# A hybrid decoder step: the samples' memory steps issued in pairs, key products in four banks

## The chip, the cores and the metric

One core of a Trainium2 chip runs the whole program. The metric is the device time in microseconds (us) of one execution. Three runs of the kernel before gave 851.37, 853.22 and 853.85 us; the median is 853.22.

## The reference, cut to what matters

One inference layer: an mLSTM branch (4 heads of 256) and a forgetting-attention branch (8 heads of 128) side by side, merged by gates, then a mixture of 32 experts. It serves a prompt of 256 tokens and 8 samples of 8 new tokens each. All data are float32. What the change touches is the mLSTM chunk of the samples. For each of 8 samples and 4 heads there is a state C (256 x 256) with a normaliser column n, held together as 256 x 257:

```python
s   = einsum('bhtd,bhsd->bhts', q, k) * w_intra
num = w_inter[..., None] * einsum('bhtd,bhde->bhte', q, C) + einsum('bhts,bhse->bhte', s, v)
C_new = decay_state[..., None, None] * C + einsum('bhs,bhsd,bhse->bhde', w_rows, k, v)
n_new = decay_state[..., None] * n + einsum('bhs,bhsd->bhd', w_rows, k)
```

For each (sample, head): the old state is multiplied by 8 queries, and a new state is the decayed old one plus the product of 8 keys with 8 values. New states are an output.

## The kernel before, in words

TensorE first computes all projections as "dense units". A unit is half of a block of 256 weight columns over 8 slices of the contraction, with each operand split in a high and a low part: 24 matmuls (for a third unit of some blocks 16), into one of banks 0 to 2. The list `SECTIONS` gives the order of the blocks: `mo mk mq mv ga gb fk fq fv bm bf out`, four each. Small stages are hung behind the units by `stages()` (line 76): the list at `(c, u)` names the stages that every engine runs after that unit. Each engine walks the same lists in its own loop and skips stages in which it has no part, so one list sets the order of work on TensorE, ScalarE and VectorE.

Stages around the change, which lie behind the last `ga` unit and the eight `gb` units:

- `SB(h, b)`: one memory step, head h, sample b; n = 8 h + b counts them, 0 to 31. TensorE multiplies the laid-out queries of the sample (`qm`) by the loaded state `Cin[n % 4]`, two column tiles of 64 output rows, into bank 5, which sums over all 8 samples of the head (the query product, L1893). Then it multiplies the sample's masked keys `kwm[n % 2]` (made by ScalarE in `keys_of_step`, L950) by the values, two row tiles of 64, one into bank 6 and one into bank 7 (the key product, L1904). VectorE adds each bank to the decayed old state (L1363, two instructions), signals `cout_full` by a memset (L1365), and the bank is free after its instruction. GpSimd then issues the load of the state of step n + 4 (L663) and the store of the new one (L675).
- At b = 7 TensorE also makes the within-sample product (L1899) into bank 4 between query and key product. VectorE lays the queries of the next head (L1349), and after its step adds the two halves of bank 5 (L1368, which frees the bank) and writes the numerator (L1371).
- `SA(h, 0)`: scores of a head (L1832) into bank 3; VectorE weighs them (L1342); ScalarE copies the head's values and keys (L941, L943).
- `F1`, `F3`, `F2`, `F2H`, `F2L`: norm, gating, transposes and splitting of a finished numerator; for the second prompt tile (t = 1) `F2H` transposes a half into bank 3 (L1873), VectorE gates it (L1322), ScalarE takes the high part (L931), and `F2L` is VectorE's low part (L1329).

In each of these lists the block's own split (ScalarE L798 high part, VectorE L1131 low part, for the block after next) comes after the steps. A bank is handed back and forth by two counts, `bank_full` and `bank_free`; `banks_of(st)` (line 128) lists which banks a stage fills, in the order of the counts, and `claim(st, b)` makes TensorE wait until the fill before has been read. SP only loads weights, gated by finished splits; at the end the expert weights stream in as their slots come free.

Of the kernel before, what the change touches and what calls it, by code (L numbers as in the profile page):

```python
# [31 lines left out]
NS = BS * TS  # L32
# [41 lines left out]
def stages():  # L74

    order = [(c, u) for c in range(NCH) for u in range(units_of(c))]
    at = {cu: [] for cu in order}

    def after(section, chunk, unit, n=0):

        return at[order[order.index((CPS * SECTIONS.index(section) + chunk, unit)) + n]]

    for n in range(1, 6):
        after("mo", 0, 1, 1 + 3 * (n - 1)).append(("G", n, 0))
    for t in range(3):
        after("mq", 1 + t, 1).append(("KT", t, 0))

    for h in range(HM):
        after("mv", h, 2, 2 if h < HM - 1 else 1).append(("P2", 0, h))
        after("mv", h, 2).append(("P1", 0, h))  # L90
    after("ga", 0, 0).append(("F1", 0, 0))
    for h in range(HM):
        after("ga", 1, 1, h).append(("P2", 1, h))
        after("ga", 0, 1, h).append(("P1", 1, h))
    after("ga", 0, 1).append(("F3", 0, 0))
    after("ga", 1, 0).append(("F2", 0, 0))

    after("ga", 2, 1).append(("SA", 0, 0))
    after("ga", 3, 0).append(("F1", 1, 0))
    for h in range(HM):  # L100
        for b in range(BS):
            line = after("ga", 3, 1, (h * BS + b) * 9 // (HM * BS))
            line.append(("SB", h, b))
            if h == 0 and b in (4, 5, 6):
                line.extend({4: (("F2H", 1, 0),), 5: (("F2L", 1, 0), ("F2H", 1, 1)), 6: (("F2L", 1, 1),)}[b])
        if h < HM - 1:
            line.append(("SA", h + 1, 0))
    after("ga", 3, 1).append(("F3", 1, 0))
    after("fk", 0, 0).append(("F1", 2, 0))
    after("fk", 0, 1).append(("F3", 2, 0))  # L110
    after("fk", 1, 0).append(("F2", 2, 0))

    for w, section in enumerate(("fk", "fq")):
        for t in range(3):
            after(section, 3, 2, 2 * t).append(("N1", w, t))
            after(section, 3, 2, 2 * t + 3).append(("N2", w, t))

    after("fv", 2, 2).append(("FS0", 0, 0))
    for n in range(HF + 2):
        line = after("fv", 3, 0, n) if n else after("fv", 2, 2)  # L120
        line.extend((k, n - s, 0) for s, k in ((2, "FS3"), (1, "FS2"), (0, "FS1"), (-1, "FS0")) if 0 <= n - s < BS)
        line.extend((k, n - s, 0) for s, k in ((2, "FP3"), (1, "FP2"), (0, "FP1")) if 0 <= n - s < HF)
        if n >= 2:
            line.append(("FS4", n - 2, 0))
    return at


def banks_of(st):

    kind, x, y = st  # L130
    if kind == "G":
        return {1: (3,), 2: (4, 5, 6), 3: (3, 7), 4: (3, 7, 4, 5, 6), 5: (3,)}[x]
    if kind == "P2":
        return (4, 6, 7) if x == 0 else (5, 4, 6, 7)
    if kind == "SB":
        return ((5, 4) if y == BS - 1 else ()) + (6, 7)
    return {"KT": (6, 7), "P1": (3,), "F1": (), "F3": (), "F2": (6, 7), "F2H": (3,), "F2L": (), "SA": (3,), "N1": (), "N2": (6, 7),
            "FP1": (7, 4), "FP2": (5,), "FP3": (6,), "FS1": (3,), "FS2": (5,), "FS3": (4,), "FS4": (3,), "FS0": ()}[kind]


# [17 lines left out]
def hybrid_step(nc, A, O):  # L158
# [10 lines left out]
    with ctx:  # L169
        handles = {}  # L170

        def sem(name):
            if name not in handles:
                
                handles[name] = ctx.enter_context(nc.semaphore(name))
            return handles[name]
# [600 lines left out]
        def _(act):  # L777
# [158 lines left out]
            def SA(st):  # L936
                h = st[1]
                n = 2 * HM + h
                pe_past(("P2", 1, HM - 2 + h) if h < 2 else ("SB", h - 2, BS - 1))
                act.wait_ge(sem("low_added"), n_low(first("mv") + h + 1))  # L940
                s(A_(vx2[NS:2 * NS, h, :], vx2[0:NS, h, :], ACT.Copy))  # L941
                for k in range(2):
                    s(A_(kw[n % 2][NS * k:NS * (k + 1), 0:P], kM(2, h)[:, P * k:P * (k + 1)], ACT.Copy,  # L943
                         scale=ew[0:NS, 2, 8 + h:9 + h]), sem("kw_ready") if k else None)
                keys_of_step(h * BS)

            def keys_of_step(n):
                if n >= 2:
                    pe_past(("SB", (n - 2) // BS, (n - 2) % BS))
                s(A_(kwm[n % 2][:, 0:P], kw[n // BS % 2][:, 0:P], ACT.Copy, scale=blk8[:, n % BS:n % BS + 1]),  # L950
                  sem("kwm_ready"))

            def SB(st):
                _, h, b = st
                if b < BS - 1:
                    keys_of_step(h * BS + b + 1)
                else:
                    got(st, 5)
                    act.wait_ge(sem("inter_used"), HM + h)
                    s(A_(inter[0:NS, :], bank[5][NS:2 * NS, 0:DE], ACT.Copy), sem("inter_upper"))  # L960
# [150 lines left out]
        def _(dve):  # L1111
# [207 lines left out]
            def gated(st, i, b):  # L1319
                t = st[1]  # L1320
                got(st, b)
                done(TT(cube(hv, 4)[:, :, 0:ROWS[t]], cube(bank[b][:, :], 4)[:, :, 0:ROWS[t]], sgm[half_of_gates(t, i)],  # L1322
                        ALU.mult), b)
                s(v.memset(small[0:1, 94:95], 0.0), sem("hv_full"))
# [4 lines left out]
                s(TT(r2[1][w], cube(hv, 4)[:, :, 0:ROWS[t]], r2[0][w], ALU.subtract), sem("ha_split"))  # L1329

            def F2H(st):
                gated(st, st[2], 3)

            def F2L(st):
                gate_lo(st[1], st[2])
# [16 lines left out]
            def SB(st):  # L1352
                _, h, b = st
                n = h * BS + b
                if n >= NCOUT:

                    dve.wait_ge(sem(f"cout_out{n % NCOUT}"), 16 * (n // NCOUT))
                if b == BS - 1 and h < HM - 1:
                    got(st, 5)
                    lay_queries(h + 1)  # L1360
                for k, bk in enumerate((6, 7)):
                    got(st, bk)
                    done(STT(Cout[n % NCOUT][:, k, :], Cin[n % NCIN][:, k, :], dec8[:, HM * b + h:HM * b + h + 1],  # L1363
                             bank[bk][:, 0:DE], ALU.mult, ALU.add), bk)
                s(v.memset(small[0:1, 94:95], 0.0), sem("cout_full"))  # L1365
                if b == BS - 1:
                    dve.wait_ge(sem("inter_upper"), h + 1)
                    TT(inter[0:NS, :], bank[5][0:NS, 0:DE], inter[0:NS, :], ALU.add).then_inc(sem("bank_free5"), 1)  # L1368
                    dve.wait_ge(sem("bank_free5"), fill[st, 5] + 1)
                    got(st, 4)  # L1370
                    done(STT(num[0:NS, h, :], inter[0:NS, :], ew[0:NS, 2, h:h + 1], bank[4][0:NS, 0:DE],  # L1371
                             ALU.mult, ALU.add), 4)
                    s(v.memset(small[0:1, 94:95], 0.0), sem("num_full"))
                    s(v.memset(small[0:1, 94:95], 0.0), sem("inter_used"))
# [319 lines left out]
        def _(pe):  # L1694
# [3 lines left out]
            def claim(st, b):  # L1698

                if fill[st, b]:  # L1700
                    pe.wait_ge(sem(f"bank_free{b}"), fill[st, b])
# [173 lines left out]
                full(ins, b)  # L1875

            def F2H(st):
                gate_turns(st, st[2], 3)

            def SA(st):  # L1880
                _, h, _ = st
# [3 lines left out]
            def SB(st):  # L1885
                _, h, b = st
                n = h * BS + b
                if b == 0:
                    claim(("SB", h, BS - 1), 5)
                    pe.wait_ge(sem("qm_full"), 2 * (h + 1))  # L1890
                pe.wait_ge(sem(f"cin_in{n % NCIN}"), 16 * (n // NCIN + 1))
                for k in range(2):
                    ins = mm(bank[5][NS * k:NS * (k + 1), 0:DE], qm[:, 576 * k + 64 * b:576 * k + 64 * (b + 1)],  # L1893
                             Cin[n % NCIN][:, k, :], start=(b == 0), stop=(b == BS - 1), skip_group_check=True)
                if b == BS - 1:
                    full(ins, 5)
                    pe.wait_ge(sem("bank_free3"), fill[("SA", h, 0), 3] + 1)
                    claim(st, 4)
                    full(mm(bank[4][0:NS, 0:DE], SW[(2 * HM + h) % 2][0:NS, 0:64], vx(2, h), start=True, stop=True), 4)  # L1899
                pe.wait_ge(sem("kwm_ready"), n + 1)  # L1900
                for k, bk in enumerate((6, 7)):
                    claim(st, bk)
                    rows = slice(NS * k, NS * (k + 1))
                    full(mm(bank[bk][:, 0:DE], kwm[n % 2][rows, 0:P], vx2[rows, h, :], start=True, stop=True), bk)  # L1904
# [333 lines left out]
```

## Time and profile before

| | |
|---|---|
| median of three runs | 853.22 us |
| the profiled execution | 851.17 us |
| its span | 849.3 us |
| TensorE busy | 738.6 us, 87% |
| VectorE busy | 403.8 us, 48% |
| ScalarE busy | 298.3 us, 35% |
| GpSimd busy | 144.2 us, 17% |
| TensorE's mean granted clock | 0.965 of full |

The span is the time from the first to the last instruction. Busy times of different engines overlap. The chain that ended last names, step by step back from the end, the work on which the next thing waited; its shares say where the time lies, while busy shares only say how much each engine did. The memory steps lie between 205.5 and 288.4 us.

### The profile page before, as it was taken

How to read it: one execution, taken by the hardware profiler on the slowest of the kernel's cores; microseconds unless marked ns; L12 is line 12 of the kernel's file. 1: busy time of each engine (PE TensorE's matmuls, PEld its weight loads, DVE VectorE, ACT ScalarE, POOL GpSimd, SP SyncE). 2: the span in 40 equal slices, each digit the busy share in tenths (PEclk: the TensorE clock that was granted, in tenths of full speed). 3: DMA queues.
4: the chain of work that ended last, by engine and by line, in shares of the span. 5: the costliest groups of instructions: out<-in, count | busy, mean ns of one | idle time of the engine just before them, and what ended most of it. 6: DMA issues, size and time to landing. Idle time of an engine off the chain costs nothing.

```text
span 849.3 us, 14573 instructions
## 1 busy us (share of the span) xinstructions
PE 738.6 (87%) x5476; PEld 592.1 (70%) x5476; DVE 403.8 (48%) x936; ACT 298.3 (35%) x550; POOL 144.2 (17%) x245
## 2 busy tenths in 40 slices
PE   2999899999999999987789999893899999777770
PEld 1799899998666798986678889882755555443430
DVE  3476233565755457584456657746642222111123
ACT  4532644465533445563222234544311111111110
POOL 5001000002433200421212100003012222212210
PEclk9999999999999999999999999997899999999995
DMA  5244343334889632736566538856399999999976
GB/s 189 100 150 144 142 141 108 102 105 183 247 247 255 219 108 104 257 101 208 178 223 227 162 109 304 352 232 237 155 421 418 419 418 418 420 419 419 419 304 193
DMA packets 38170, 202.84 MB, mean 239 GB/s; under 512 B 7490, under 2 KB 8018, under 8 KB 18898
## 3 DMA queue, kind: packets, MB, share of 16 engines
q1 hardware_dynamic: 24434, 160.29, 49.3%
q0 software_dynamic: 13664, 41.58, 15.5%
q8 instruction: 46, 0.75, 0.4%
q14 instruction: 26, 0.21, 0.1%
HBM read 184.24 MB, written 23.38 MB: 244 GB/s over the span
## 4 chain that ended last, share of the span: by engine, by line
PE 60%; DMA 18%; DVE 11%; ACT 5%; issue 4%; SPq 1%; POOLq 0%; DVEq 0%; POOL 0%; ACTq 0%
PE bank L1742 20%; PE bank L1746 10%; DMA fm<-in_w_moe 7%; DMA em<-in_w_moe 7%; PE bank L2096 6%; PE bank L1732 3%; PE bank L2116 3%; DVE rm L1131 2%; PE bank L1904 2%; ACT rm L798 2%; PE bank L1988 2%; PE bank L2077 2%; PE bank L1893 1%; DMA fm<-y_rows 1%; DMA fm<-in_w_dense 1%
## 5 line engine op out<-in xcount | busy, mean ns | idle before, releaser
L1742 PE MATMUL bank<-rm 128*128 128x320 f32 x1344 | 206.0, 312 | 2.6 <-ACT fm L826 1.6
L1742 PEld LDWEIGHTS bank<-rm 128*128 128x128 f32 x1344 | 197.4, 188 | 7.0 <-issue 3.1
L1131 DVE TENSOR_TENSOR rm<-fm,rm 128x2048 fp32r<-128x2048 f32 x48 | 110.0, 2292 | 71.8 <-ACT rm L798 71.2
L1746 PE MATMUL bank<-rm 128*128 128x256 f32 x960 | 122.3, 287 | 2.4 <-DVE fm L1522 2.4
L1746 PEld LDWEIGHTS bank<-rm 128*128 128x128 f32 x960 | 118.4, 194 | 3.3 <-issue 2.9
L798 ACT ACTIVATE rm<-fm 128x2048 fp32r<-128x2048 f32 x48 | 91.9, 1915 | 19.0 <-PE bank L1742 11.1
L2098 PE MATMUL bank<-fm,em 128*64 128x256 f32 x384 | 96.6, 397 | 0.0
L2096 PE MATMUL bank<-em 128*64 128x256 f32 x272 | 68.1, 395 | 13.4 <-DMA fm<-in_w_moe 7.9
L2096 PE MATMUL bank<-fm,em 128*64 128x256 f32 x240 | 58.9, 390 | 10.6 <-DMA fm<-in_w_moe 9.2
L2096 PEld LDWEIGHTS bank<-em 128*64 128x64 f32 x272 | 36.2, 141 | 40.4 <-issue 25.3
L1094 ACT ACTIVATE fm<-bank 64x256 f32<-64x256 f32 x32 | 12.0, 375 | 136.7 <-PE bank L2098 136.7
L732 POOL DMA_INDIRECT y_rows<-fm,im x32 | 29.2, 913 | 161.7 <-DVE fm L1648 157.4
L2096 PEld LDWEIGHTS bank<-fm,em 128*64 128x64 f32 x240 | 31.6, 139 | 33.5 <-issue 18.7
L2098 PEld LDWEIGHTS bank<-fm,em 128*64 128x64 f32 x384 | 51.4, 141 | 0.0
L663 POOL DMA_DIRECT2D fm<-in_state_C x32 | 17.6, 551 | 164.4 <-DVE fm L1284 119.1
L1653 DVE TENSOR_TENSOR fm<-bank,fm 64x256 f32<-64x256 f32 x32 | 13.6, 426 | 61.7 <-ACT fm L1094 61.6
L1732 PE MATMUL bank<-rm 128*128 128x256 f32 x320 | 42.9, 286 | 0.0
L1363 DVE SCALAR_TENSOR_TENSOR fm<-fm,bank 128x257 f32<-128x257 f32 x64 | 28.0, 479 | 30.4 <-PE bank L1904 29.5
L1660 DVE COPY fm<-bank 128x128 f32<-128x128 f32 x32 | 9.3, 291 | 68.3 <-PE bank L2107 68.2
L1732 PEld LDWEIGHTS bank<-rm 128*128 128x128 f32 x320 | 40.0, 192 | 1.6 <-DVE fm L1522 1.5
L1648 DVE COPY fm<-bank 64x512 f32<-64x512 f32 x32 | 22.2, 694 | 29.5 <-PE bank L2116 29.5
L1087 ACT ACTIVATE fm<-bank 64x512 f32<-64x512 f32 x32 | 18.9, 589 | 44.7 <-PE bank L2116 44.7
(391 smaller groups left out, 1013.4 us busy)
## 6 DMA issues: line engine op xcount, KB each, us to landing
fm<-in_w_moe SPq DMA_DIRECT2D x57, 1024.0 KB, 26.8
fm<-in_w_dense SPq DMA_DIRECT2D x48, 1024.0 KB, 4.9
em<-in_w_moe SPq DMA_DIRECT2D x39, 1024.0 KB, 26.0
fm<-in_state_C POOLq DMA_DIRECT2D x32, 257.0 KB, 5.4
out_C_sample<-fm POOLq DMA_DIRECT2D x32, 257.0 KB, 6.5
fm<-in_cache_v POOLq DMA_DIRECT2D x16, 512.0 KB, 4.5
fm<-in_cache_kT POOLq DMA_DIRECT2D x10, 512.0 KB, 5.8
em<-in_cache_kT POOLq DMA_DIRECT2D x6, 512.0 KB, 7.9
```

Of the source, the lines that this page charges most:

```text
L732: pool.indirect_dma_start(y_rows, bass.IndirectOffsetOnAxis(ap=row_i[:, v:v + 1].bitcast(U32), axis=0), yrow[v % NY], None, bounds_check=6 ...
L798: s(A_(pair[c % 2][0], cube(raw[c % RAW1], KC), ACT.Copy), sem("hi_done"))
L1087: A_(yrow[v % NY][:, 0:D // 2], bank[4 + v % 2][0:CAP, :], ACT.Copy).then_inc(sem("e_y_left"), 1)
L1131: s(TT(pair[c % 2][1], cube(raw[c % RAW1], KC), pair[c % 2][0], ALU.subtract), sem("split_done"))
L1363: done(STT(Cout[n % NCOUT][:, k, :], Cin[n % NCIN][:, k, :], dec8[:, HM * b + h:HM * b + h + 1], bank[bk][:, 0:DE], ALU.mult, ALU.add), bk)
L1648: CP(yrow[v % NY][:, D // 2:D], bank[4 + v % 2][CAP:2 * CAP, :]).then_inc(sem("e_y_right"), 1)
L1732: ins = mm(bank[b][:, 0:CW], samp[:, k, :], w[:, k, :], start=(k == 0 and i == 0), stop=(k == KC - 1 and i == 1))
L1742: ins = mm(bank[b][:, 0:NT], w[:, k, P * u:P * (u + 1)], a[:, k, :], start=first, stop=final)
L1746: ins = mm(bank[b][0:r, 0:CW], a[:, k, TILE0[u]:TILE0[u] + r], w[:, k, :], start=first, stop=final)
L2096: last_g = mm(bank[b][0:CAP, 0:FE], x[:, k, :], g[:, k, :], start=(k == 0), stop=(k == KC - 1), skip_group_check=True)
L2098: last_u = mm(bank[b][CAP:2 * CAP, 0:FE], x[:, k, :], u[:, k, :], start=(k == 0), stop=(k == KC - 1), skip_group_check=True)
L2116: ins = mm(bank[b][CAP * j:CAP * (j + 1), :], hT[:, k, :], w[:, k, 512 * j:512 * (j + 1)], start=(k == 0), stop=(k == 1), skip_group_check ...
```

## The change

Three edits that hang together:

1. In the lists, the two steps of a pair (b even and b + 1) now always stand behind the same dense unit. TensorE runs the query products of both at the even step; the odd step has only its key product. At the end of a head the sum in bank 5 and the within-sample product thus come at b = 6, ahead of both last key products.
2. Key products use banks 6 and 7 for even steps, 3 and 4 for odd ones, and 3 and 6 for b = 7.
3. The scores and copies of the next head (`SA`) come after b = 3 and not after b = 7; the masked keys of a head's first step are made by the step before it. `F2H` moves ahead of the step b = 4 with its first half, its second half uses bank 4.

```diff
-            line = after("ga", 3, 1, (h * BS + b) * 9 // (HM * BS))
+            line = after("ga", 3, 1, (h * BS + b // 2 * 2) * 9 // (HM * BS))
+            if h == 0 and b == 4:
+                line.append(("F2H", 1, 0))
             line.append(("SB", h, b))
-            if h == 0 and b in (4, 5, 6):
-                line.extend({4: (("F2H", 1, 0),), 5: (("F2L", 1, 0), ("F2H", 1, 1)), 6: (("F2L", 1, 1),)}[b])
-        if h < HM - 1:
-            line.append(("SA", h + 1, 0))
+            if h == 0 and b in (4, 5):
+                line.extend({4: (("F2L", 1, 0), ("F2H", 1, 1)), 5: (("F2L", 1, 1),)}[b])
+            if h < HM - 1 and b == 3:
+                line.append(("SA", h + 1, 0))
...
+KEY_BANKS = [(6, 7), (3, 4)] * 3 + [(6, 7), (3, 6)]
...
     if kind == "SB":
-        return ((5, 4) if y == BS - 1 else ()) + (6, 7)
+        return ((5, 4) if y == BS - 1 else ()) + KEY_BANKS[y]
+    if kind == "F2H":
+        return (3 + y,)
...
-                keys_of_step(h * BS)
+                if h == 0:
+                    keys_of_step(0)
...
-                if b < BS - 1:
+                if h * BS + b + 1 < HM * BS:
                     keys_of_step(h * BS + b + 1)
-                else:
+                if b == BS - 1:
...
-                pe.wait_ge(sem(f"cin_in{n % NCIN}"), 16 * (n // NCIN + 1))
-                for k in range(2):
-                    ins = mm(bank[5][NS * k:NS * (k + 1), 0:DE], qm[:, 576 * k + 64 * b:576 * k + 64 * (b + 1)],
-                             Cin[n % NCIN][:, k, :], start=(b == 0), stop=(b == BS - 1), skip_group_check=True)
-                if b == BS - 1:
+                for c in (b, b + 1) if b % 2 == 0 else ():
+                    m = h * BS + c
+                    pe.wait_ge(sem(f"cin_in{m % NCIN}"), 16 * (m // NCIN + 1))
+                    for k in range(2):
+                        ins = mm(bank[5][NS * k:NS * (k + 1), 0:DE], qm[:, 576 * k + 64 * c:576 * k + 64 * (c + 1)],
+                                 Cin[m % NCIN][:, k, :], start=(c == 0), stop=(c == BS - 1), skip_group_check=True)
+                if b == BS - 2:
                     full(ins, 5)
                     pe.wait_ge(sem("bank_free3"), fill[("SA", h, 0), 3] + 1)
-                    claim(st, 4)
+                    claim(last, 4)
                     full(mm(bank[4][0:NS, 0:DE], SW[(2 * HM + h) % 2][0:NS, 0:64], vx(2, h), start=True, stop=True), 4)
                 pe.wait_ge(sem("kwm_ready"), n + 1)
-                for k, bk in enumerate((6, 7)):
+                for k, bk in enumerate(KEY_BANKS[b]):
```

With this the steps behind the nine units are 0-3, 4-7, 8-11, 12-15, 16-17, 18-21, 22-25, 26-29, 30-31; before they are 0-3, 4-7, 8-10, 11-14, 15-17, 18-21, 22-24, 25-28, 29-31.

## Rows read from the trace of the kernel before

**Rows 1.** The page: busy time of TensorE, and the chain's shares.
```profile
PE 738.6 (87%) x5476; PEld 592.1 (70%) x5476; DVE 403.8 (48%) x936; ACT 298.3 (35%) x550; POOL 144.2 (17%) x245
...
PE 60%; DMA 18%; DVE 11%; ACT 5%; issue 4%; SPq 1%; POOLq 0%; DVEq 0%; POOL 0%; ACTq 0%
PE bank L1742 20%; PE bank L1746 10%; DMA fm<-in_w_moe 7%; DMA em<-in_w_moe 7%; PE bank L2096 6%; PE bank L1732 3%; PE bank L2116 3%; DVE rm L1131 2%; PE bank L1904 2%; ACT rm L798 2%; PE bank L1988 2%; PE bank L2077 2%; PE bank L1893 1%; DMA fm<-y_rows 1%; DMA fm<-in_w_dense 1%
```

**Rows 2.** Stretches: length, busy PE, PEld, DVE, ACT, POOL, clock, DMA share, GB/s.
```profile
205.47:288.33 82.86, 78.90 (x477) 51.18 (x476) 46.63 (x135) 33.92 (x63) 32.00 (x59) 1.00 0.86 255
...
211.36:223.10 11.74, 11.02 (x71) 6.95 (x71) 10.74 (x28) 7.61 (x13) 5.04 (x10) 1.00 0.87 257
223.10:231.22 8.12, 7.95 (x50) 5.52 (x48) 3.80 (x15) 3.51 (x8) 2.61 (x6) 1.00 0.96 233
231.22:240.95 9.73, 9.45 (x57) 6.23 (x57) 5.79 (x14) 3.14 (x6) 4.33 (x9) 1.00 0.87 247
240.95:251.01 10.06, 8.76 (x56) 5.81 (x55) 4.37 (x17) 4.37 (x9) 3.25 (x7) 1.00 0.89 273
251.01:260.67 9.66, 9.49 (x57) 6.31 (x57) 5.78 (x14) 2.84 (x6) 4.33 (x9) 1.00 0.79 242
260.67:270.19 9.52, 8.70 (x55) 5.80 (x55) 4.13 (x16) 4.48 (x9) 3.96 (x8) 1.00 0.89 241
270.19:279.86 9.67, 9.50 (x59) 6.31 (x57) 5.92 (x14) 2.72 (x6) 3.62 (x7) 1.00 0.93 260
279.86:288.33 8.47, 8.29 (x51) 5.49 (x50) 2.50 (x9) 2.25 (x5) 2.34 (x5) 1.00 0.66 223
```

**Rows 3.** The chain of waits in a clean stretch: start, length, what.
```profile
251.08 3.72 PE bank L1742 x24
254.80 0.58 PE bank L1893 x4
255.38 0.64 PE bank L1904 x3
...
256.14 0.49 DVE fm L1363
...
256.77 1.00 PE bank L1904 x4
```

**Rows 4.** The timeline at a head's end, ScalarE and VectorE.
```profile
246.28 0.84 ACT L943 ACTIVATE fm<-fm 64x128 f32<-64x128 f32 x2
...
246.63 0.87 DVE L1363 SCALAR_TENSOR_TENSOR fm<-fm,bank 128x257 f32<-128x257 f32 x2 [0.74 <-PE bank L1904]
...
247.56 0.42 DVE L1368 TENSOR_TENSOR fm<-bank,fm 64x257 f32<-64x257 f32 x1
```

**Rows 5.** The chain of waits elsewhere: five products of TensorE.
```profile
200.73 0.43 PE bank L1855 x2
...
216.37 0.60 PE bank L1873 x4
...
222.80 0.38 PE bank L1832 x4
...
245.32 0.57 PE bank L1899 x2
...
444.55 1.90 PE bank L1953 x16
```

**Rows 6.** The timeline in the second stretch, VectorE.
```profile
214.31 2.29 DVE L1131 TENSOR_TENSOR rm<-fm,rm 128x2048 fp32r<-128x2048 f32 x1 [0.24 <-DVE fm L1307]
...
217.57 0.69 DVE L1322 TENSOR_TENSOR fm<-bank,fm 128x512 f32<-128x512 f32 x1
```

**Rows 7.** Loads of the state (L663): whole program, then 229 to 243 us.
```profile
  PEld bank L1893: 0.5, 1
...
DMA to landing us min/median/max: 3.4/5.4/7.5
...
DMA to landing us min/median/max: 3.4/6.8/7.3
```

More of the change, by code:

```diff
@@ L135, in banks_of @@
     if kind == "SB":
-        return ((5, 4) if y == BS - 1 else ()) + (6, 7)
-    return {"KT": (6, 7), "P1": (3,), "F1": (), "F3": (), "F2": (6, 7), "F2H": (3,), "F2L": (), "SA": (3,), "N1": (), "N2": (6, 7),
+        return ((5, 4) if y == BS - 1 else ()) + KEY_BANKS[y]
+    if kind == "F2H":
+        return (3 + y,)
+    return {"KT": (6, 7), "P1": (3,), "F1": (), "F3": (), "F2": (6, 7), "F2L": (), "SA": (3,), "N1": (), "N2": (6, 7),
             "FP1": (7, 4), "FP2": (5,), "FP3": (6,), "FS1": (3,), "FS2": (5,), "FS3": (4,), "FS4": (3,), "FS0": ()}[kind]
@@ L1331, in F2H @@
             def F2H(st):
-                gated(st, st[2], 3)
+                gated(st, st[2], 3 + st[2])
             def F2L(st):
@@ L1877, in F2H @@
             def F2H(st):
-                gate_turns(st, st[2], 3)
+                gate_turns(st, st[2], 3 + st[2])
             def SA(st):
@@ L1887, in SB @@
                 n = h * BS + b
+                last = ("SB", h, BS - 1)
                 if b == 0:
-                    claim(("SB", h, BS - 1), 5)
+                    claim(last, 5)
                     pe.wait_ge(sem("qm_full"), 2 * (h + 1))
-                pe.wait_ge(sem(f"cin_in{n % NCIN}"), 16 * (n // NCIN + 1))
-                for k in range(2):
-                    ins = mm(bank[5][NS * k:NS * (k + 1), 0:DE], qm[:, 576 * k + 64 * b:576 * k + 64 * (b + 1)],
-                             Cin[n % NCIN][:, k, :], start=(b == 0), stop=(b == BS - 1), skip_group_check=True)
-                if b == BS - 1:
+                for c in (b, b + 1) if b % 2 == 0 else ():
[5 more added lines that the diff above has]
+                if b == BS - 2:
                     full(ins, 5)
                     pe.wait_ge(sem("bank_free3"), fill[("SA", h, 0), 3] + 1)
-                    claim(st, 4)
+                    claim(last, 4)
                     full(mm(bank[4][0:NS, 0:DE], SW[(2 * HM + h) % 2][0:NS, 0:64], vx(2, h), start=True, stop=True), 4)
                 pe.wait_ge(sem("kwm_ready"), n + 1)
-                for k, bk in enumerate((6, 7)):
+                for k, bk in enumerate(KEY_BANKS[b]):
                     claim(st, bk)
```

## The prediction

> **What bounds the kernel now.** I read the page's busy row and chain first [rows 1]: TensorE is busy 87% of the span and owns 60% of the chain of waits; the expert weights' transfers own 14%, all at the end. Then the busy times by stretch [rows 2]. The edit lies between 205.47 us (first memory step) and 288.33 us (first `fk` unit), 82.86 us, in which TensorE is busy 78.90 at full granted clock, VectorE 46.63, ScalarE 33.92, GpSimd 32.00; the transfer engines are 86% busy. So TensorE's program order sets the time here, and the transfers come next. What lies behind is started by events of TensorE (units done, slots used), the expert weights too, so I pass a change of this stage to the end one for one.
>
> The stage is nine runs of steps with eight dense units between them. A clean dense unit takes 3.72 us: its 24 matmuls start at 251.08 and the next query product at 254.80 [rows 3]. A step's query product takes 0.58 us of TensorE, its key product 0.64 if both banks are free [rows 3]. The clean stretch 251.01 to 260.67 has one unit and four steps, 3.72 + 4 x 1.22 = 8.60, but takes 9.66: 1.06 is waiting. The chain shows on whom: key product at 255.38, VectorE starts on its bank 0.76 later (I use 0.80, from the start), and 0.63 after VectorE's start (256.14 to 256.77) the next key product starts, on the first bank alone; the second follows, so it takes 1.00 and not 0.64 [rows 3]. In all: 8 x 3.72 + 32 x 1.22 + 4 x 0.57 (within-sample products) + 3 x 0.38 (scores) + 2 x 0.60 (transposes of F2H) [rows 5] = 73.4; so 9.4 of 82.86 are waits or lost overlap. That is what can be won.
>
> **What the change removes and adds.** The counts of all products, evacuations and transfers stay; two copies per head change place. I walk TensorE through the nine stretches with these prices:
> - Step of VectorE: 0.94 from one to the next if nothing holds it (246.63 to 247.56 [rows 4]). It frees its first bank 0.63 after its start, its second at about 1.01.
> - Second of two query products back to back. The trace of before has no such pair. Bounds: 0.58 as today, and 0.43, the time of two instructions of the full array and the same width [rows 5]. The nearest row is FS1: sixteen instructions of 264 columns in two alternating column tiles in 1.90 us, 0.475 per four [rows 5]. Scaled to 257 columns: 0.46. I take 0.46, and for the second key product 0.50 (bounds 0.43 and 0.64).
> - Scores in mid-head: 0.38, but they claim bank 3, which the step before (odd, banks 3 and 4) has just filled. From the key product of step 2 VectorE needs 0.80 + 0.94 + 0.63 = 2.37 until that bank is free.
> - Last step of a head: banks 3 and 6. Bank 6 was filled by step 6, so from step 6's key product: 0.80 + 0.63 = 1.43, then 0.55 for a half product alone: 1.98 where 1.14 would do.
>
> The walk; a clean pair is 0.58 + 0.46 + 0.64 + 0.50 = 2.18.
> 1. Steps 0 to 3: 2.18, then 1.04, wait 2.37, scores 0.38: 5.97. Before 5.89 (205.47 to 211.36 [rows 2]; so for the others).
> 2. Steps 4 to 7: unit 3.72, turn 0.60, queries 1.04, key 4 at 5.36, turn to 6.60. Step 5 needs bank 4, which the second turn filled. VectorE: its 2.29 us split ended 5.24 into this stretch; ScalarE now does the next head's three copies (0.84 for two [rows 4], 1.26) ahead of its table load, and that load starts 0.70 later against the unit than today, so the split ends at 5.94. Then gating 0.69, a memset, step 4 (0.94), the low half 0.69, gating 0.69 [rows 6]: 9.1, with gaps and signal 9.3. Key 5 ends at 9.85. Queries 1.04, within-sample 0.57, keys 1.98: 13.44. Before 11.74.
> 3. Steps 8 to 11 and scores: 3.72 + 5.97 = 9.69. Before 8.12 with three steps.
> 4. Steps 12 to 15: 3.72 + 2.18 + 1.04; the within-sample product claims bank 4 of step 13, free at 3.72 + 1.04 + 0.80 + 0.94 + 1.01 = 7.51; 0.57; 1.98: 10.06. Before 9.73.
> 5. Steps 16, 17: 3.72 + 2.18 = 5.90. Before 10.06 with three steps, the scores and the head's edge.
> 6. Steps 18 to 21, scores between: 3.72 + 1.04 + 2.37 + 0.38 + 2.18 = 9.69. Before 9.66.
> 7. Steps 22 to 25, a head's edge inside: key 22 at 3.72 + 1.04 + 0.57 = 5.33. Bank 5 is free after 0.80, step 0.94, query copies 0.45, step 0.94, sum 0.42, 0.14: at 9.02; then 2.18: 11.20. Before 9.52.
> 8. Steps 26 to 29: 3.72 + 4.36 = 8.08. Before 9.67.
> 9. Steps 30, 31: 3.72 + 1.04 + 0.57 + 1.98 = 7.31. Before 8.47.
> Sum 81.34 against 82.86: **-1.5 us**. The clean stretches win 1.6 each; scores in mid-head, the head's last step, the turn in bank 4 and the one head's edge without a dense unit behind it give most of it back.
>
> **Loads of the state.** Four buffers: the load of step n+4 is issued once VectorE has finished step n. Today loads land 3.4 to 7.5 us after issue, 5.4 in the median, and TensorE waits 0.5 for one of them [rows 7]. In a clean stretch of today the need comes 9.66 - 0.58 - 0.80 - 0.94 - 0.3 (GpSimd's start) = 7.0 after issue. In the walk the odd step's query product comes earlier and its buffer doesn't. Example, step 17: VectorE ends step 13 at 3.72 + 1.04 + 0.80 + 0.94 + 0.94 = 7.44 of stretch 4, GpSimd issues at 7.9 (it still issues step 12's store), and the need is 10.06 - 7.9 + 3.72 + 0.58 = 6.5 later; loads of that time took up to 7.3 [rows 7], so it waits 0.8. In the same way step 9 has 6.8 where 7.5 was needed (0.7), step 10 has 5.8 + 0.7 against 6.8 (0.3), step 31 has 4.6 against 5.4 (0.8); today's wait stays (0.4). Sum 3.0, less the 0.5 that is there already: **+2.5**. Bounds: -0.5 (every load in time) and +4.2 (each 0.5 us slower, felt at three or four places, as the engines are 86% busy already).
>
> The Trainium skill (DMA: Bandwidth & Descriptors, Anatomy of one DMA) fits a transfer on GpSimd's path as about 2.0 us plus the bytes at 436 GB/s. For 257 KB an estimate by that page is 2.6 us, the loads would all be in time and the sum would be -2.0. The trace doesn't agree: 5.4 in the median [rows 7], with stores and dense weights on the same engines, so I go by the rows.
>
> **Sum.** -1.5 + 2.5 = +1.0 us on the profiled execution's 851.17 (span 849.3, 1.9 around it): 852.2. That execution lies 2.0 below the median of the runs shown; the same difference on the median 853.22 gives 854.2. A measurement of this kernel tells 0.3%, 2.6 us, from no change; this is within it. Costs taken as nothing: ScalarE's masked copies (0.4 each, like those in [rows 4]) keep ahead of the key products, since each needs only the product two steps back; without that cover a pair would lose some 0.2. GpSimd's queue has the same 60 issues.
>
> The 0.12 and 0.14 that I gain at each second product also follow from a rule of the Trainium skill (TensorEngine Tiling (Array Packing), Key Properties): changing the tiling mode drains TensorE. Query products use column tiles, key products row tiles, so pairing halves the changes. The rule gives no price, and no run so far shows such a pair.
>
> **Rivals.**
> - Loads in time and part of the new waits absent (faster). For: only one load wait today, and my bank waits are stacked one on the other. Against: walked with the same prices, today's clean stretch comes out at 9.6, and is 9.66 [rows 2]. The new bank waits of the walk are 3 x 1.2 (scores), 4 x 0.8 (last steps) and 2.6 (turn in bank 4), 9.4; with a fifth of them gone, -1.5 - 0.5 - 2.0 = -4.0: 849.2. Chance 0.22.
> - The state's transfers decide (slower). Place: the odd query product of a pair, behind which the even step's key product, ready long ago, is queued. It decides where a load takes over some 6 us. Each 0.5 us more of latency costs 1.7: +4.2 - 1.5 = +2.7 at 0.5 more, +4.4 at 1.0; I take +4.0: 857.2. For: 86% busy, latencies up to 7.5. Against: the stage has no more bytes than before and, waiting, gives them time. Chance 0.18.
> - Back-to-back products gain nothing (slower): the 16 second queries lose 0.12 and the eight second keys that nothing else holds 0.14, so +3.0 on the forecast: +4.0, also 857.2. Against: the FS1 row. Chance 0.12.
> - The forecast: 0.48, its own range 851.5 to 856.5.
>
> Faster is the first rival, 0.22; slower the second and third, 0.30; same 0.48. The range for 8 in 10 takes most of both sides: 850.0 to 858.0.
>
> **What would show it.** Right: the eighth stretch at 8.1 for four steps; scores starting about 2.4 after the key product of step 2; the key product of a head's last step taking 1.3 or more; the stretch of steps 4 to 7 longer than 13; three or more waits of query products for `in_state_C`, together 2 to 3 us; in pairs a second query product 0.46 behind the first. Wrong: a stage of 79 or less (the new waits are not there), or over 86 with load waits above 4; a change of more than 1 us outside the stage would make passing it on one for one wrong.

## The result: slower, 863.96 us, and the profile after

Four runs of the changed kernel gave 858.92, 863.43, 864.49 and 867.66 us, median 863.96, against 852.5 for the kernel before beside it: a ratio of 1.0128, 95% interval 1.0086 to 1.0169. The forecast was 854.2, range 850.0 to 858.0. The profiled execution took 864.49, 13.3 more than the 851.17 of before: the stage begins 1.25 earlier, is 13.65 longer, and what lies behind it takes 561.9 for 561.0. The earlier begin need not come of the change: the profiles of runs in the order of before begin the stage between 203.4 and 205.5.

In the page TensorE's busy time has grown by 4.9 with the same 5476 matmuls [rows 1]:

```profile
PE 743.5 (86%) x5476; PEld 597.9 (69%) x5476; DVE 406.0 (47%) x936; ACT 298.5 (35%) x550; POOL 143.9 (17%) x245
...
PE 57%; DMA 19%; DVE 12%; ACT 5%; issue 5%; SPq 1%; POOL 1%; POOLq 0%; DVEq 0%; ACTq 0%
```

The stretches after (columns as in [rows 2]), first the whole stage, then the nine behind the nine units. The last columns are granted clock, DMA share and GB/s.

```profile
204.22:300.73 96.51, 82.43 (x478) 56.55 (x477) 48.94 (x136) 35.20 (x63) 31.33 (x58) 0.88 0.73 219
204.22:210.00 5.78, 4.88 (x38) 2.80 (x37) 4.49 (x16) 3.35 (x9) 2.70 (x6) 1.00 0.90 314
210.00:226.21 16.21, 14.31 (x68) 8.69 (x67) 10.75 (x28) 8.30 (x12) 4.27 (x8) 0.76 0.81 245
226.21:236.85 10.64, 9.77 (x61) 7.60 (x61) 5.34 (x18) 3.36 (x9) 4.34 (x9) 0.88 0.52 134
236.85:252.50 15.65, 11.66 (x60) 7.12 (x58) 6.11 (x16) 4.25 (x7) 4.29 (x9) 0.79 0.85 246
252.50:259.90 7.40, 7.40 (x41) 6.29 (x40) 1.92 (x8) 1.06 (x3) 1.67 (x4) 0.76 0.52 143
259.90:269.25 9.35, 8.19 (x62) 6.19 (x60) 6.31 (x15) 5.18 (x10) 4.33 (x8) 1.00 0.63 194
269.25:283.33 14.08, 11.03 (x60) 6.90 (x59) 5.58 (x20) 2.83 (x8) 4.33 (x8) 0.88 0.78 240
283.33:293.42 10.09, 8.11 (x58) 5.79 (x57) 5.67 (x13) 3.56 (x6) 4.33 (x8) 1.00 0.71 226
293.42:300.73 7.31, 7.07 (x45) 5.17 (x43) 2.78 (x10) 3.30 (x5) 1.08 (x2) 1.00 0.72 206
```

The walk had 5.97, 13.44, 9.69, 10.06, 5.90, 9.69, 11.20, 8.08, 7.31. Where the clock is 1.00 and no load is waited for (first, sixth, ninth) it holds within 0.4. The excess stands in the other six, and two things share it. One is late loads: TensorE's waits in the stage (engine, line, releaser: us, times, longest) have 7.1 us for `in_state_C`. The kernel before has no such wait of a product, only one of a weight load, 0.5 [rows 7]; weight loads wait 9.3 here.

```profile
PE bank L1904 <- DMA fm<-in_state_C: 7.1, 4, 3.2
PE bank L1840 <- DVE fm L1371: 2.9, 3, 1.2
PE bank L1904 <- DVE fm L1376: 1.7, 1, 1.7
PE bank L1915 <- ACT fm L958: 1.4, 1, 1.4
```

The timeline shows the longest being made. GpSimd issues four loads (L670) and four stores (L682) back to back; the fourth load, step 15's, is the one that step 15's query product (L1904) waits for:

```profile
234.11 0.55 POOL L670 DMA_DIRECT2D fm<-in_state_C  x1 [5.79 <-DVE fm L1373]
...
237.40 0.55 POOL L670 DMA_DIRECT2D fm<-in_state_C  x1
237.94 0.54 POOL L682 DMA_DIRECT2D out_C_sample<-fm  x1
...
243.54 0.65 PE L1904 MATMUL bank<-fm 128*64 128x257 f32 x4 [0.82 <-DMA fm<-in_state_C]
...
247.36 1.12 PE L1904 MATMUL bank<-fm 128*64 128x257 f32 x4 [3.16 <-DMA fm<-in_state_C]
```

The trace's landing time of that one load alone:

```profile
DMA to landing us min/median/max: 9.9/9.9/9.9
```

The other is TensorE's clock. The last row of the timeline has four matmuls in 1.12 us, where the row above it has step 14's same four in 0.65. Windows of 2 us show the granted clock fall in or behind a pause (in each the busy time of TensorE stands behind the length, the clock third from the end):

```profile
216.00:218.00 2.00, 0.63 (x5) 0.39 (x5) 1.85 (x6) 1.03 (x2) 0.16 (x1) 1.00 0.66 113
218.00:220.00 2.00, 1.47 (x4) 0.62 (x4) 1.51 (x4) 0.76 (x2) 0.93 (x2) 0.63 0.95 242
220.00:222.00 2.00, 2.00 (x9) 0.77 (x8) 1.23 (x3) 0.68 (x2) 0.72 (x2) 0.50 0.92 380
...
246.00:248.00 2.00, 0.64 (x4) 0.30 (x4) 0.00 (x0) 0.00 (x0) 0.00 (x0) 0.50 0.87 308
248.00:250.00 2.00, 2.00 (x8) 0.79 (x6) 0.00 (x0) 0.00 (x0) 0.00 (x0) 0.50 0.96 390
```

0.50 is 1.2 GHz, 1.00 is 2.4 GHz. The fall comes three times in the stage: from 218.6 to 228.9 (behind a pause of 1.4 us and in one of 0.5), from 245.8 to 256.2 (it falls within the load wait of 3.2), from 279.8 to 283.4 (behind the head's edge, 1.7). The stage of before is at 1.00 throughout.

### The profile page after: what moved, and what is told of

Read it like the earlier page. It is cut to its first block, busy times and chain, and to the rows that moved or that the text cites. A ratio compares the mean times of both kernels' runs of the same rounds, so it can differ in the third digit from the quotient of the medians.

```text
span 862.6 us, 14573 instructions
## 1 busy us (share of the span) xinstructions
PE 743.5 (86%) x5476; PEld 597.9 (69%) x5476; DVE 406.0 (47%) x936; ACT 298.5 (35%) x550; POOL 143.9 (17%) x245
## 4 chain that ended last, share of the span: by engine, by line
PE 57%; DMA 19%; DVE 12%; ACT 5%; issue 5%; SPq 1%; POOL 1%; POOLq 0%; DVEq 0%; ACTq 0%
PE bank L1750 19%; PE bank L1754 10%; DMA fm<-in_w_moe 7%; DMA em<-in_w_moe 7%; PE bank L2107 6%; PE bank L1740 3%; PE bank L2127 3%; DMA fm<-in_state_C 3%; DVE rm L1139 3%; ACT rm L805 2%; PE bank L1915 2%; PE bank L1999 2%; PE bank L2088 2%; PE bank L1904 1%; DMA fm<-y_rows 1%
## 5 line engine op out<-in xcount | busy, mean ns | idle before, releaser
L1750 PE MATMUL bank<-rm 128*128 128x320 f32 x1344 | 208.8, 314 | 2.6 <-ACT fm L833 1.6
L2109 PE MATMUL bank<-fm,em 128*64 128x256 f32 x384 | 98.1, 401 | 0.0
L2107 PE MATMUL bank<-fm,em 128*64 128x256 f32 x240 | 63.1, 410 | 14.2 <-DMA fm<-in_w_moe 12.8
L2107 PE MATMUL bank<-em 128*64 128x256 f32 x272 | 65.3, 383 | 8.4 <-DMA fm<-in_w_moe 4.8
L2107 PEld LDWEIGHTS bank<-fm,em 128*64 128x64 f32 x240 | 33.1, 146 | 38.8 <-issue 24.2
L2109 PEld LDWEIGHTS bank<-fm,em 128*64 128x64 f32 x384 | 51.8, 142 | 0.0
L670 POOL DMA_DIRECT2D fm<-in_state_C x32 | 17.5, 548 | 177.5 <-DVE fm L1292 119.1
```

What stands on the lines that cost most here:

```text
L1750: ins = mm(bank[b][:, 0:NT], w[:, k, P * u:P * (u + 1)], a[:, k, :], start=first, stop=final)
L2107: last_g = mm(bank[b][0:CAP, 0:FE], x[:, k, :], g[:, k, :], start=(k == 0), stop=(k == KC - 1), skip_group_check=True)
L2109: last_u = mm(bank[b][CAP:2 * CAP, 0:FE], x[:, k, :], u[:, k, :], start=(k == 0), stop=(k == KC - 1), skip_group_check=True)
```

## The experiments

The table has, for the profiled execution, the stretch from the first query product to the first `fk` unit, and all executions' median. "Pauses" are those of TensorE of 1.2 us or more in the stage, with a star where the clock fell to 0.50 in the pause or within 3 us behind it. The ratio is to the runs of the kernel before that were timed beside each run (medians 852.4 to 852.8), not to the 853.22 of the first row.

| kernel | stage us | PE busy | clock | DMA | pauses | median (range) | ratio to before, interval |
|---|---|---|---|---|---|---|---|
| before | 82.86 | 78.90 | 1.00 | .86 | none | 853.22 (851.4-853.9) | |
| after | 96.51 | 82.43 | .88 | .73 | 1.4* 3.2* 1.7* 2.0 | 863.96 (858.9-867.7) | 1.0128, 1.0086-1.0169 |
| e1 | 84.18 | 73.82 | .98 | .86 | 1.4 1.2* 1.7 | 856.00 (850.6-863.1) | 1.0046, 1.0011-1.0082 |
| e2 | 88.64 | 81.33 | .90 | .81 | 1.3* 2.4* 1.2* | 854.44 (852.2-857.1) | 1.0025, 1.0008-1.0041 |
| e3 | 87.81 | 82.34 | 1.00 | .81 | none | 860.55 (859.7-864.5) | 1.0109, 1.0072-1.0145 |
| e4 | 82.79 | 78.93 | 1.00 | .86 | none | 852.29 (850.6-854.3) | 1.0006, 0.9991-1.0020 |
| e5 | 87.47 | 79.74 | .92 | .80 | 2.8* 3.5* | 854.85 (852.3-857.7) | 1.0019, 1.0003-1.0034 |
| e6 | 86.36 | 77.27 | .98 | .84 | 2.4 2.3* | 854.96 (847.5-858.7) | 1.0017, 0.9992-1.0042 |
| e7 | 83.03 | 78.83 | 1.00 | .84 | none | 852.53 (850.4-854.0) | 0.9993, 0.9977-1.0009 |
| e8 | 87.58 | 80.90 | .96 | .81 | 2.8* | 858.83 (858.6-860.1) | 1.0075, 1.0047-1.0103 |
| e9 | 80.53 | 72.29 | 1.00 | .90 | 1.4 1.7 | 854.65 (849.1-861.2) | 1.0030, 1.0003-1.0058 |
| e10 | 80.50 | 76.22 | .98 | .89 | 1.7* | 847.48 (843.7-850.9) | 0.9942, 0.9920-0.9964 |
| e11 | 80.52 | 72.30 | 1.00 | .53 | 1.4 1.7 | 851.51 (847.8-854.4) | 0.9985, 0.9961-1.0008 |
| e12 | 82.82 | 78.96 | 1.00 | .50 | none | 851.27 (850.0-853.4) | 0.9993, 0.9979-1.0008 |
| e13 | 77.10 | 74.32 | 1.00 | .56 | none | 846.01 (844.9-846.3) | 0.9927, 0.9907-0.9946 |
| e14 | 83.64 | 76.35 | .99 | .87 | 2.4* | 855.49 (852.9-861.0) | 1.0041, 1.0022-1.0059 |
| e15 | 85.36 | 80.02 | .98 | .83 | 1.5* | 855.18 (853.6-857.9) | 1.0044, 1.0025-1.0064 |
| e16 | 80.76 | 75.63 | 1.00 | .51 | none | 851.35 (849.0-854.0) | 0.9982, 0.9967-0.9996 |
| e17 | 78.11 | 74.08 | 1.00 | .87 | none | 848.17 (847.0-849.9) | 0.9950, 0.9933-0.9968 |

**e1, e4: six state buffers**, in the changed kernel and in the one before.

```diff
-NCIN, NCOUT = 4, 4
+NCIN, NCOUT = 6, 4
...
-            s(CP(dg[0:16, 0, 0:NT], bank[7][0:16, 0:NT]), sem("gates_taken"))
+            s(CP(dg[0:16, 0, 0:NT], bank[7][0:16, 0:NT]), sem("wg_split"))
```

(Not shown: the new buffers' places in memory. Two early counts, `gates_taken` and `lfn_ready`, give up their semaphores. All runs with more buffers have this.)

> The changed kernel with six buffers for the loaded states in place of four, so that a load is issued two steps earlier. In the changed kernel the memory stage takes 96.5 us, with 8.0 us of waits of query products for loads, and the granted clock of TensorE in it is 0.88 in the mean (0.50 in three spells). Theory A (pauses of TensorE, of whatever cause, are followed by spells at half clock, and these are the larger part of the loss): load waits go to under 1 us, the spell at 246 us goes with its pause, the one at 218 us, which follows a wait for the transposes' bank, stays; stage 83 to 87 us, whole 850 to 856 us. Rival B (the new waits on banks alone are the loss): the loads don't matter, 861 to 865 us. Rival C (the clock falls for a reason outside the stage, such as heat or the other work of the chip): load waits go, the clock stays near 0.88, 856 to 859 us.

> The kernel before with six buffers for the loaded states. It waits once for a load, 0.5 us. All theories: 852 to 854 us, stage 82.3 to 83 us, clock 1.00. If it gains more than 2 us, loads bound the stage in a way that the waits don't show, and the first kernel's reading is wrong.

e4 takes the time of the kernel before: loads don't bound it. In e1 no load is late and the median falls by 8 of the 11.5 that were lost, so most of the loss hung on late loads (its A, at the upper end). One thing of A missed: the pause of 1.4 at step 5 stayed, and no spell at half clock came behind it. What comes in place of late loads is late stores; VectorE's waits:

```profile
DVE fm L1372 <- DMA out_C_sample<-fm: 7.4, 2, 5.0
```

**e2: the four key banks alone**, in the order of before: `KEY_BANKS = [(6, 7), (3, 4)] * 3 + [(6, 7), (6, 7)]`.

> The kernel before with one part of the change alone: odd steps' key products in banks 3 and 4, but b = 7 in banks 6 and 7; the order of products, steps and scores as before. Theory A: clean stretches of four steps shrink from 9.66 to about 8.7 us, no pause over 1.5 us, clock stays 1.00, stage 79 to 81 us, whole 849 to 851.5 us. Rival B (four banks bring waits on banks 3 and 4 that cost what they save): stage 82 to 85, whole 852 to 856. Rival D (the loads bind once steps are faster): stage 81 to 84 with load waits of 2 us or more.

Each clean four-step group loses its bank waits (4.88 us from 204.20 to 209.08), yet the stage grows: 3.2 us of waits for `in_state_C` and three stretches at half clock. Theory D had the load waits, none the clock.

**e3: the changed kernel with twenty idle identity products in its five pauses.**

> The changed kernel with idle products (identity times a constant table, 256 columns, 0.43 us each, overwritten by the next real product) put into five of its pauses: 3 ahead of the key product of step 5, 7 between the query products of steps 14 and 15, 2 between 22 and 23, 4 between 28 and 29, 4 ahead of step 24; 20 in all, 8.7 us of work that is of no use. Theory A (idle pauses bring the half clock): the clock in the stage is 0.97 or more, stage 86 to 89 us, whole 853 to 857 us, though TensorE has more to do. Rival B or a loss that comes of the waits alone: the products at best fill pauses, stage 96 to 99 us, whole 864 to 867 us. Rival C (clock falls for another reason): as B.

The clock of the stage is 1.00 and the stage is 8.7 shorter, as A had it; the whole is only 3.4 better and missed A's range, since behind the stage it took 566.2 for 561.9.

**e5, e6: both cures together**, other banks with six buffers, and pairs with six buffers and idle products (`mm(bank[b][:, 0:256], ident, negs, ...)`).

> The order of the kernel before (no pairs, scores and copies at the head's edge), with six state buffers instead of four, and key products of odd steps in banks 3 and 4 wherever TensorE made no extra pause of over 1 us for them: steps 4 to 7 of the first head and every head's last step stay in banks 6 and 7. Theory A (TensorE loses time beyond its own waits where a pause of 1 us or more is followed by half the granted clock; short bank waits only cost themselves): no pause over 1 us is left but the turn of the first head, granted clock of the stage 0.98 or more, stage 76 to 79.5 us, whole 846 to 850. Theory B (the banks bring nothing, since VectorE's pace takes the place of TensorE's waits): stage 81.5 to 83.5, whole 851.5 to 854. Theory C (the loads again): query products wait for in_state_C over 2 us in sum, whole 852 or more.

> The changed kernel with six state buffers, and seven idle identity products of 256 columns into banks 3 and 7, three ahead of the key product of step 5 and four ahead of step 24, so that TensorE is at work in the two places where it paused for over 1 us. Their results are not used. Theory A (the changed kernel's excess over the walk is half clock after pauses, and late loads): with both gone the stage is 82 to 85 us at a granted clock of 0.98 or more, whole 851.5 to 855. Theory B (the walk itself was too short: pairs, scores in mid-head and the head's last step cost more than their waits): stage 86 or more at full clock, whole 856 or more.

No theory of e5 fits: its stage is 87.47, with no wait of TensorE for a load. Of e6 the median is in A's range, its stage of 86.36 is not. Both fail at one place, the store. VectorE's waits in e5 and, second, in e6:

```profile
DVE fm L1353 <- DMA out_C_sample<-fm: 5.1, 1, 5.1
DVE fm L1367 <- DMA out_C_sample<-fm: 1.5, 2, 0.9
```

```profile
DVE fm L1372 <- DMA out_C_sample<-fm: 14.2, 3, 6.4
```

With loads far ahead, a step waits until the state of four steps ago is stored. In e5 TensorE then pauses 2.8 and 3.5 us, and the clock falls with each; in e6 it pauses 2.4 and 2.3, and the clock falls only at the second.

**e7, e15, e8: one pause of TensorE alone**, in e4's kernel, by 3, 5 and 7 copies on ScalarE ahead of step 20's masked keys.

```diff
+                if (h, b) == (2, 3):
+                    for _ in range(3):
+                        s(A_(hv, hv, ACT.Copy))
```

> The kernel before with six state buffers and three copies of a masked half onto itself added on ScalarE (0.6 us each) ahead of the masked copies of step 20, so that one key product of TensorE comes about 2 us late, in a stage that runs at full granted clock otherwise. Theory A (a pause of 1 to 3 us may be followed by some 10 us at half the granted clock): in the executions in which that happens the time rises by the pause and some 4 to 5 us more, in the others by the pause alone; the profile shows 0.50 in the windows behind it, or nothing; whole 853 to 859, with more spread than before. Theory B (a pause costs its own length and no clock): whole 852.5 to 855 in every run, clock 1.00 behind the pause.

> The kernel before with six state buffers and five copies on ScalarE ahead of step 20's masked copies; three made no pause of TensorE beyond 0.2 us, seven made one of 2.8. Here it is about 1.5. Theory A (a pause of this size is followed by half clock in some executions and not in others): the executions fall around 853 to 854 (852.3 and the pause less what the next wait gives back) and around 857, the median between. Theory B (it takes over 2 us of pause): all at 852.5 to 855.

> As the run with three copies, with seven: one pause of TensorE of about 4.4 us. Theory A: the half clock behind it comes in more of the executions, or in all: whole 857 to 863, of which 4.4 is the pause. Theory B: 855.5 to 858, the pause alone, clock 1.00 behind it. If the time is that of the run with three copies, the copies are hidden behind something and the run says nothing on the clock.

Three copies make no pause (0.17) and cost nothing, so e7 tells nothing of the clock. Five make one of 1.50 and cost 2.8 over before; the seven executions lie at 853.6 to 855.2 (four) and 857.4 to 857.9 (three). Seven copies make one of 2.82 and cost 6.3, in all four executions. Of e8, TensorE's timeline behind the pause and two windows in it:

```profile
259.63 1.23 PE L1908 MATMUL bank<-fm 64*128 64x257 f32 x4 [2.82 <-ACT fm L952]
260.79 1.13 PE L1897 MATMUL bank<-fm 128*64 128x257 f32 x4
```

```profile
256.00:258.00 2.00, 0.81 (x6) 0.20 (x4) 0.88 (x3) 1.91 (x4) 1.65 (x4) 1.00 0.85 262
...
260.00:262.00 2.00, 2.00 (x10) 0.59 (x8) 0.88 (x3) 0.42 (x2) 0.00 (x0) 0.50 0.57 210
```

Against e4 the profiled stage is 2.57 longer in e15 (1.09 of it is busy time) and 4.79 longer in e8 (1.97 of it busy), so within the stage a pause cost 1.7 times its length. By the medians it is 1.8 and 2.2 times; the rest lies outside the stage and was not traced to the pause. Nor are e15's two groups those with and without the fall: the profiled execution, 855.13, is of the lower group and has it. This is the only place where one pause was varied with order and transfers as they were.

**e9, e10: five buffers for loads and five for stores**, for the changed kernel and for the order of before with the other banks.

```diff
-NCIN, NCOUT = 4, 4
+NCIN, NCOUT = 5, 5
+KEY_BANKS = [[(6, 7), (3, 4)] * 2 + [(6, 7)] * 4] + [[(6, 7), (3, 4)] * 3 + [(6, 7), (6, 7)]] * 3
```

(`KEY_BANKS` in e10 alone. Not shown: the list of slots, in which a store's buffer is not always n % 5, and a wait of ScalarE for the last store from the fifth.)

> The changed kernel with five buffers for loaded states and five for states to be stored (before: four and four). With six and four, VectorE waited up to 5 us for a store (out_C_sample) ahead of a step and TensorE then paused over 1 us. Theory A (late loads and late stores make the long pauses, and half clock follows some of them): waits for in_state_C and out_C_sample together under 3 us, stage 82 to 86 us, whole 852 to 857. Theory B (the fifth buffer only moves the wait, since the transfers can't follow in this stage): waits for transfers of 4 us or more in sum, stage 86 or more, whole 857 or more.

> The order of the kernel before, key products of odd steps in banks 3 and 4 except at a head's last step and steps 4 to 7, and five buffers each for loads and stores. With six and four this had two pauses of 2.8 and 3.5 us behind waits for stores and lost 6.8 us to the half clock behind them; without both its stage would be 76 to 77. Theory A: the fifth output buffer takes most of these waits away: stage 76 to 80, whole 846.5 to 850. Theory B (the stage's transfers can't be done in less than about the 82.8 us of before, the buffers only shift where it is felt): stage 82 to 86, whole 852 to 856, with waits for transfers of 4 us or more.

e9's profile has one wait of VectorE for a store left, 4.4 us, hidden from TensorE, and a stage of 80.53 at full clock, shorter than both theories; its median is in A's range. Its executions spread from 849 to 861, the longer ones at a lower mean clock (0.959 for 849.1, 0.949 for 861.2). e10's median is A's, its stage of 80.50 just above; it is 5 us faster than before and the fastest of the kernels that move whole states. Against e10 the pairs and what goes with them (e9) cost 7.2 us in the median. Five and five buffers in the kernel before alone were not run.

**e11, e12, e13: half of every state moved**, with four buffers each; the changed kernel, the kernel before, and the other banks.

```diff
+                w = slice(0, 1 if n >= NCIN else 2)
-                pool.dma_start(Cin[n % NCIN], A["state_C"][n % BS, n // BS])
+                pool.dma_start(Cin[n % NCIN][:, w], A["state_C"][n % BS, n // BS][:, w])
```

> The changed kernel with half of every state loaded and stored from step 4 on (the other half is left out of the outputs; all products and evacuations stay). Theory A (late transfers cause the load waits, and they and the pause of step 5 the spells at half clock): no wait for in_state_C, stage 81 to 85.5 us (the walk of 81.3, with at most one spell behind the pause of 1.4 us at step 5), whole 850 to 855. Theory B (the order of the products itself is slow): stage 88 or more, whole 857 or more.

> The same with the kernel before, as its control. TensorE sets its stage and no transfer is late in it: stage 82.3 to 83, whole 851.5 to 853.5, by both theories. If it comes out faster by over 1 us, transfers held the kernel before as well.

> The kernel before with four buffers each, key products of odd steps in banks 3 and 4 except at a head's last step and steps 4 to 7, and half of every state loaded and stored from step 4 on (the other half is missing in the outputs). Theory A (only late transfers held the other banks back): no wait for a transfer, stage 80 to 81 us as with five buffers each, whole 845 to 849. Theory B (the fifth buffers did something else): stage 82 or more, whole 850 or more.

With its program order untouched and less to move, the changed kernel has no transfer wait and its median is 12.5 us lower, so it was slow by transfers that come late under its order, and not by the order's own length. That of the kernel before is 1.2 lower, by its expectation a sign that transfers held it too; but its stage is the same (82.82), and the interval takes in no change. e11's stretches, the DMA share now 0.53:

```profile
204.09:284.61 80.52, 72.30 (x478) 51.65 (x477) 48.97 (x136) 35.21 (x63) 31.34 (x58) 1.00 0.53 174
204.09:209.85 5.76, 4.89 (x38) 2.92 (x37) 4.50 (x16) 3.35 (x9) 2.68 (x5) 1.00 0.88 333
209.85:223.13 13.28, 11.14 (x69) 7.42 (x67) 10.28 (x27) 8.29 (x12) 3.79 (x8) 1.00 0.63 211
223.13:232.62 9.49, 8.62 (x61) 6.45 (x60) 5.82 (x19) 3.36 (x9) 4.83 (x9) 1.00 0.25 86
232.62:242.82 10.20, 9.20 (x61) 6.34 (x59) 5.64 (x15) 4.25 (x7) 3.81 (x8) 1.00 0.67 219
242.82:248.62 5.80, 5.80 (x42) 4.70 (x41) 2.41 (x9) 1.07 (x3) 2.16 (x4) 1.00 0.39 113
248.62:257.97 9.35, 8.18 (x63) 6.19 (x61) 6.31 (x15) 5.18 (x10) 4.33 (x8) 1.00 0.57 190
257.97:269.13 11.16, 9.22 (x61) 6.34 (x59) 5.15 (x19) 2.43 (x7) 4.33 (x8) 1.00 0.47 118
269.13:277.31 8.18, 8.18 (x59) 6.14 (x57) 6.39 (x15) 4.14 (x7) 3.53 (x7) 1.00 0.52 176
277.31:284.61 7.30, 7.06 (x44) 5.16 (x43) 2.48 (x9) 3.13 (x4) 1.88 (x4) 1.00 0.40 142
```

e13 shows what the banks alone are worth when nothing is late: a stage of 77.10, 5.7 under e12's (and shorter than its A), and 5.3 in the median. The changed kernel under the same terms (e11) is 3.4 longer in the stage and 5.5 in the median: its reordering costs more than it gives.

**e14, e16: idle products in the pauses** at step 5 and at step 24, in e9's and in e11's kernel.

> The changed kernel with five buffers each and seven idle identity products of TensorE, three ahead of the key product of step 5 and four ahead of step 24, in its two pauses of 1.4 and 1.7 us. Theory A (the half clock in most executions of the run without them comes from these pauses): stage 80.5 to 82 in the profile, whole 847 to 851, and a smaller spread than 849.1 to 861.2. Theory B (the half clock has nothing to do with the pauses): median 853 to 856 and the same spread as without.

> The changed kernel with half of every state loaded and stored from step 4 on (the other half is missing in the outputs), so that no transfer is late, and the seven idle products of TensorE, three ahead of the key product of step 5 and four ahead of step 24. Without them the executions lay at 847.8 to 848.3, 851.0 to 852.9 and 854.0 to 854.4, median 851.5, by the mean granted clock of each. Theory A (the pauses of 1.4 and 1.7 us bring the half clock of the upper two groups): all executions at 847.5 to 850. Theory B (the half clock comes from elsewhere): the same groups and a median of 851 to 853.

e14 came out in B's range but says little: a 6.8 us wait for a store is back and makes a pause of 2.4. e16 went by B: no pause over 1.2 is left in its stage, and the executions still lie at 849.0 to 854.0. So the spread of e11 doesn't come from those two pauses.

**e17: e10 with stores issued ahead of loads.**

> The order of before with the other key banks and five buffers each (847.5 us), with each store issued ahead of the load of five steps later and not behind it. Theory A (a store lands later by what the load ahead of it takes, the loads have time to spare with five buffers): waits of VectorE for out_C_sample under 1 us in sum, whole 845 to 848. Theory B (the loads now come late instead): waits for in_state_C over 1 us, whole 848 to 852.

No store is waited for, one load for 0.9, the stage is 2.4 shorter than e10's in the profile, but the whole is the same: 848.17 against 847.48, the ranges overlap.

## Why the prediction was wrong

- **The walk held.** With no transfer late, e11's stage has 80.52 for the forecast 81.34; its stretches 5.76, 13.28, 9.49, 10.20, 5.80, 9.35, 11.16, 8.18, 7.30 lie within 0.35 of it each. Scores start 2.28 behind the key product of step 2 (2.4 forecast); a pair of query products takes 1.02 and one 0.58, so the second 0.44; a pair of key products 1.07 and one 0.64, so 0.43 (0.46 and 0.50 forecast). The rival "gains nothing" falls. One cost taken as nothing, ScalarE's masked keys, did show: the pause of 1.37 ahead of step 5 ends with them (L958). It hid behind the wait for bank 4, 0.53 more, so the length came out right; but it is the pause right behind which the clock first fell in the changed kernel.
- **Of the -1.5 nothing reached the median.** e11 against e12 is 851.5 to 851.3, though the profiled stages differ by 2.3. Passing the stage on one for one was too simple: behind it the 19 profiled executions took 560.7 to 566.2, with other stretches at half clock. Of e11's 565.5 against e12's 560.7, 3.0 us are busy time of TensorE (480.4 against 477.4); e11 has half clock from 326.5 to 330.5 and from 395.0 to 398.5, where e12 has none. Whether the stage brings that or chance was not settled.
- **The load term: forecast +2.5, 7.1 us of waits measured.** The mechanism was right (query products of steps 14, 15, 23 and 29 wait, three of them the second of a pair), the size was not, and the steps named (9, 10, 17, 31) were not those. I took latencies of up to 7.5 from a trace in which four loads spread over 4.6 us, from 237.55 to 242.14. Here four are issued in 3.3 us, from 234.1 to 237.4, each with its store, and the fourth takes 9.9. The pitch alone doesn't explain it: four loads issued in the same 3.3 us from 207.2 on take 4.7 to 6.9. Beside the 9.9 a weight block of 1 MB was under way, beside the 6.9 none; no run varied the two apart. The bound of +4.2 allowed only 0.5 us more latency.
- **The step that failed: every price was taken at full granted clock.** Against e11's stage TensorE is idle 5.9 us more (96.51 - 82.43 against 80.52 - 72.30) and busy 10.1 us more on the same products: 16.0 together. The loads' +2.5 stands against the 5.9. The busy part (for which the sum had nothing) is the half clock in and behind its pauses. No case of mine had it; "over 86 with load waits above 4" named the sign, not this price. The rival in which the transfers decide had the place and the chain, and 857.2 instead of 864 mainly for lack of the same term.
- **How far the clock's cause is shown.** e8 and e15 make one pause and lose its length and nearly as much again. e3 fills the pauses and has the clock at 1.00. Over 19 profiled stages there were 22 pauses of 1.2 us or more; behind 14 the clock fell, and in the 8 stages without one it never did. (1.2 us is no threshold: in e1 it fell at 288.3, just behind the stage, behind a pause of 1.04.) Of the pauses over 2.3 us, 7 of 8 were followed by it, of those of 1.2 to 2.0 us 7 of 14; the same pause of 1.37 at step 5 was followed by it in the changed kernel and not in e1, e9 and e11. What decides between them stays open.

The Trainium skill (TensorE: Matmul & The Clock Gate, A second HAM failure mode) tells of a kernel in which short idle times between groups of matmuls make the clock swing between its two levels. This trace agrees in part: 0.88 over the stage and 10.1 us with pauses of 1.4 to 3.2 us, while e9 and e11 kept 1.00 with two such pauses.

On the loads the Trainium skill (DMA: Bandwidth & Descriptors, Issuing engines are not separate DMA queues) says that all issuing engines share the same 16 transfer engines. This trace agrees: the late load of 9.9 us went with three other state loads, four stores and a dense block issued at 241.10.

## What to carry to other kernels

In this stage, with the transfer engines 73 to 90% busy where whole states moved, the latency of a load was no constant: before regrouping steps, count what the new order issues within one latency (loads, stores, and the weight block beside them), and give both pools (in and out) the buffers for it, since more buffers for loads alone ended the waits for loads and brought waits for stores. Price a new pause of TensorE of 1.5 to 3 us at about twice its length, as e15 and e8 measured. A reordering and a resource that it brings along deserve separate looks: the key banks with five buffers each made this kernel 0.6% faster (e10), and the pairs with their scores in mid-head took 5 to 7 us away again (e11 against e13, e9 against e10).

## What the runs showed of the hardware

- The granted clock fell behind pauses of 1.2 to 2.0 us in this stage in half of the cases. The same code is hit in one execution and not in another: at about 90 us, in dense units that no run changed, TensorE pauses 1.58 us in all 19 profiled executions, and the clock fell in 12 of them. Ten us around 97 in the changed kernel and in e3, the same code up to here (clock third from the end):

```profile
91.90:102.12 10.22, 9.20 (x63) 8.93 (x62) 4.78 (x3) 4.12 (x5) 0.00 (x0) 1.00 0.44 160
92.02:102.24 10.22, 10.22 (x62) 10.22 (x61) 4.78 (x3) 4.04 (x5) 0.00 (x0) 0.83 0.35 117
```

- e9's ten executions lie 12.0 us apart, the 31 of before that were timed beside it 4.4.
- Transfers of one size (257 KB) took from 3.3 to 9.9 us to land in one stage; the longest were issued behind three other loads with their stores, with a weight block of 1 MB under way.
